# Regrouping a layer's small products on TensorE: fourteen places instead of seventeen, and two opening units in turn

## What is computed

```python
for l in range(2):
    h = rmsnorm(x)
    q, k, v, h_b, gate_b, gate_c, qc, f, i, og, zg = split(h @ w_in)      # 50 blocks of 128 columns
    ya = dilated_attention(rope(q), rope(k), v)         # 3 groups; the samples read a cache
    yb = gate_b * conv(gate_c * h_b)
    yc = gated_linear_recurrence(qc, f, i, state) ...   # HGRN2, then head norm and silu(og)
    x = x + (g0 * (ya @ w_pa) + g1 * (yb @ w_pb) + g2 * (yc @ w_pc)) @ w_o
    x = x + square(relu(rmsnorm(x) @ w_up)) @ w_down
return rmsnorm(x), and the new caches and states
```

## Time and profile before

| | |
|---|---|
| median of 3 runs | 814.51 us (814.47 to 814.7) |
| the profiled execution | 814.41 us |
| its span, first to last instruction | 812.6 us |
| busy: PE, DVE, ACT, POOL | 803.2, 559.7, 437.9, 271.8 us |
| mean granted TensorE clock | 0.997 |

### The profile page before, as it was taken

How to read it: one execution, slowest core, us unless ns; L and a number is a source line. 1 busy time by engine, 2 the same in 40 slices (tenths; PEclk the granted TensorE clock), 3 DMA queues, 4 the chain that set the end, 5 groups by cost and what they waited for, 6 DMA issues and landing times.

```text
span 812.6 us, 17682 instructions
## 1 busy us (share of the span) xinstructions
PE 803.2 (99%) x6786; PEld 790.5 (97%) x6786; DVE 559.7 (69%) x776; ACT 437.9 (54%) x625; POOL 271.8 (33%) x246
## 2 busy tenths in 40 slices
PE   8999999999999999999999999999999999999996
PEld 8999999999999999999999999999999999999996
DVE  7979777577867665554577777866787766645552
ACT  6654566545557664444354637675455666644442
POOL 3597293055700000122139825902664000001220
PEclk9999999999999999999999999999999999999998
DMA  9898899678566688767559969987765767787761
GB/s 313 236 318 295 295 262 314 188 235 318 185 210 220 219 276 291 259 238 251 187 169 232 358 212 343 262 246 232 269 221 178 252 230 251 238 284 242 250 206 53
DMA packets 171033, 199.88 MB, mean 246 GB/s; under 512 B 19680, under 2 KB 168624, under 8 KB 169648
## 3 DMA queue, kind: packets, MB, share of 16 engines
q1 hardware_dynamic: 169040, 196.48, 74.6%
q10 hardware_dynamic: 1936, 2.61, 0.9%
HBM read 191.17 MB, written 51.90 MB: 299 GB/s over the span
## 4 chain that ended last, share of the span: by engine, by line
PE 92%; POOL 3%; DVE 3%; ACT 0%; issue 0%; ACTq 0%; DVEq 0%; POOLq 0%
PE main L690 28%; PE main L691 27%; PE main L692 27%; PE small L692 1%; PE small L691 1%; PE small L690 1%; PE small L706 1%; POOL k_lv L1738 1%; POOL cum_f L1747 1%; DVE w_lo L1270 1%; PE small L735 1%; POOL suf_f L1744 1%; PE small L749 1%; DVE h_lo L1286 0%; POOL v_cache L1728 0%; PE small L782 0%
## 5 line engine op out<-in xcount | busy, mean ns | idle before, releaser
L1025 ACT ACTIVATE w_hi<-raw 128x1024 fp32r<-128x1024 f32 (+1 forms) x256 | 266.4, 1042 | 237.7 <-PE main L692 152.9
L1270 DVE TENSOR_TENSOR w_lo<-raw,w_hi 128x1024 fp32r<-128x1024 f32 (+1 forms) x256 | 330.7, 1293 | 65.5 <-ACT w_hi L1025 64.3
L690 PE MATMUL main<-h_hi,w_hi 128*128 128x264 f32 x1248 | 358.6, 287 | 0.1
L691 PE MATMUL main<-h_lo,w_hi 128*128 128x264 f32 x1248 | 353.7, 283 | 0.0
L692 PE MATMUL main<-h_hi,w_lo 128*128 128x264 f32 x1248 | 353.5, 283 | 0.0
L690 PEld LDWEIGHTS main<-h_hi,w_hi 128*128 128x128 f32 x1248 | 235.1, 188 | 4.0 <-issue 1.3
L691 PEld LDWEIGHTS main<-h_lo,w_hi 128*128 128x128 f32 x1248 | 235.2, 188 | 0.2
L692 PEld LDWEIGHTS main<-h_hi,w_lo 128*128 128x128 f32 x1248 | 234.0, 188 | 0.0
L690 PE MATMUL main<-a_hi,w_hi 128*128 128x264 f32 x512 | 145.3, 284 | 0.0
L691 PE MATMUL main<-a_lo,w_hi 128*128 128x264 f32 x512 | 145.0, 283 | 0.0
L692 PE MATMUL main<-a_hi,w_lo 128*128 128x264 f32 x512 | 145.0, 283 | 0.0
(11 more groups left out here) (241 smaller groups left out, 1035.9 us busy)
## 6 DMA issues: line engine op xcount, KB each, us to landing
raw<-in_w_in SPq DMA_DIRECT2D x48, 1024.0 KB, 6.4
raw<-in_w_up SPq DMA_DIRECT2D x32, 1024.0 KB, 5.3
raw<-in_w_down SPq DMA_DIRECT2D x32, 1024.0 KB, 5.4
out_kvs<-in_cache SPq DMA_DIRECT2D x48, 512.0 KB
out_kvs<-in_cache SPq DMA_DIRECT2D x32, 496.0 KB
raw<-in_w_o SPq DMA_DIRECT2D x8, 1024.0 KB, 5.8
raw<-in_w_br SPq DMA_DIRECT2D x8, 768.0 KB, 4.9
gates<-q_scratch SPq DMA_DIRECT2D x4, 768.0 KB, 8.0
```

The lines of the kernel that those rows point to most:

```text
L690: pe.matmul(out[:, 0:TOK], wh, rh, start=start and k == 0, stop=False)
L691: pe.matmul(out[:, 0:TOK], wh, rl, start=False, stop=False)
L1025: act.activation(w_hi[:, slot(l, u), 0:k, :], raw_of(u, k), ACT.Copy).then_inc(w_hi_ready, 1)
L1270: dve.tensor_tensor(w_lo[:, slot(l, u), 0:k, :], raw_of(u, k), w_hi[:, slot(l, u), 0:k, :].bitcast(F32), ALU.subtract).then_inc(w_lo_ready, 1)
```

## The change

The 17 places become 14: after units 8, 10, 12, 14, 17, 19, 21, 23, 25, 30, 32, 35, 37 and 39. Levels 7 and 8 move to place 17 (level 7 from 14, level 8 from 15), "values T" to place 14 and "recurrence" to place 19 (from 17). "Decayed keys T" moves from place 17 to place 21, ahead of the second half of the scores, and its copy on ACT from the turn of unit 18 to that of unit 22. Sample states, state, sample recurrence and the transposes of keys and values are regrouped at 21, 23 and 25; head norm and sample scores share place 30; the transposes of the probabilities go to 32. `TURNS` is written in the new order, so that the banks change too. The copy of "recurrence" moves from DVE (turn 18) to ACT (turn 20). `kv_outer` on DVE moves from turn 19 to turn 18. In the first layer, DVE computes the decays before `split_lo(7)`, not after it. In the second layer units 0 and 1 run in turn: seven row blocks of unit 0, seven of unit 1, then the last of each. SP's stores of the new keys and values move to match.

The diff, cut to its core:

```diff
+LEVELS_AT = ((10, (2, 3)), (12, (4, 5)), (14, (6,)), (17, (7, 8)))
 TURNS = (
     ["norm1"]
-    + ["values T", "sample values T"]
+    + ["sample values T"]
     + [f"first levels {hp} {h}" for hp in range(2) for h in range(2)]
-    + [f"level {i} {h}" for i in range(2, 9) for h in range(2)]
-    + ["recurrence", "decayed keys T", "state"]
-    + ["sample q T", "scores 0 0", "scores 1 0"]
-    + ["sample kv T 0", "sample kv T 1", "scores 0 1", "scores 1 1"]
-    + ["kv T 0", "sample states", "sample recurrence", "kv T 1", "kv T 2"]
-    + ["head norm 0", "head norm 1"]
+    + [f"level {i} {h}" for i in range(2, 7) for h in range(2)]
+    + ["values T"] + [f"level {i} {h}" for i in range(7, 9) for h in range(2)]
+    + ["recurrence", "sample q T", "scores 0 0", "scores 1 0"]
+    + ["decayed keys T", "scores 0 1", "scores 1 1", "sample states"]
+    + ["state", "sample recurrence", "sample kv T 0", "sample kv T 1"]
+    + ["kv T 0", "kv T 1", "kv T 2"]
+    + ["head norm 0", "head norm 1", "sample scores T"]
     + [f"probs T {i}" for i in range(4)]
...
 # PE
+            def opening(l):
+                for k0, nk in ((0, KT - 1), (KT - 1, 1)):
+                    for u in range(2):
...
+                        mm = unit(slot(l, u), main[bank_of(l, u)], h_hi, h_lo, k0, nk, wk0=k0, start=k0 == 0,
+                                  stop=k0 + nk == KT, per_k=per_k)
...
-                if u == 17:
+                if u == 19:
                     pe.wait_ge(masked, l * 20 + 20)
                     pe.wait_ge(far_ready, 2 * l + 2)
                     pe.wait_ge(v_tm_ready, l + 1)
...
                     done(mm, "recurrence")
+                    pe.wait_ge(roped, l + 1)
+                    transposes(l, "sample q T", [(g * P, z[:, CT_Q + g, PROMPT:TOK]) for g in range(NG)])
+                    scores(l, 0)
+                if u == 21:
                     pe.wait_ge(final_keys, l + 1)
                     transposes(l, "decayed keys T", [((tb * 2 + hp) * P, q_lv[:, 1, hp, tb * P:tb * P + P])
                                                      for tb in range(2) for hp in range(2)])
-                if u == 19:
+                    scores(l, 1)
+                    sample_states(l)
+                if u == 23:
                     pe.wait_ge(k_tm_ready, l + 1)
...
 # ACT
-                if u == 18:
+                if u == 22:
                     copy_bank(l, "decayed keys T", k_tm[:, :, :, :].rearrange("p t h c -> p (t h c)"),
                               lambda b: b[:, :], k_tm_ready)
                     freed("decayed keys T", k_tm_ready, l + 1)
                 if u == 20:
...
+                    copy_bank(l, "recurrence", o_c[:, :, 0:PROMPT], lambda b: b[:, :].rearrange("p (h t) -> p h t", h=2),
+                              o_prompt_ready)
...
 # DVE
                         if l == 0:
                             bounds()
                             new_params()
-                            split_lo(l, at + 4)
...
                         dve.sem_inc(kg_ready, 1)
+                        if l == 0:
+                            split_lo(l, at + 4)
...
                     if u == 20:
                         dve.wait_ge(bands_in, 16)
                         dve.wait_ge(k_tm_ready, l + 1)
                         mask_scores(0)
...
-                    if u in (10, 12, 14):
-                        mask_level(u - 8)
-                        mask_level(u - 7)
+                    for turn, numbers in LEVELS_AT:
+                        if u == turn:
+                            for i in numbers:
+                                if i < 8:
+                                    mask_level(i)
```

More of the change, by code:

```diff
@@ L772, in sample_rows, with keys_values @@
                 done(mm, "sample recurrence")
+            def keys_values(l, g):
+                transposes(l, f"kv T {g}", [((part * 2 + kv) * P, prompt_part(z[:, (CT_K, CT_V)[kv] + g, :], g, part))
+                                            for part in range(2) for kv in range(2)])
             def attend(l):
@@ L797, in norm1_squares @@
                 done(pe.matmul(bank[:, 0:TOK], ones, sq[:, :], start=False, stop=True), "norm1")
+            def opening(l):
+                for k0, nk in ((0, KT - 1), (KT - 1, 1)):
+                    for u in range(2):
+                        if k0 == 0:
+                            pe.wait_ge(w_lo_ready, l * UNITS + u + 5)
+                            pe.wait_ge(out_taken, l * OUTS + u + 1)
+                        per_k = None
+                        if u == 0:
+                            per_k = lambda k: pe.wait_ge(h_ready, l * 2 * KT + k0 + k + 1)
+                        elif k0 == 0:
+                            per_k = lambda k: norm1_squares(l) if k == 5 else None
+                        mm = unit(slot(l, u), main[bank_of(l, u)], h_hi, h_lo, k0, nk, wk0=k0, start=k0 == 0,
+                                  stop=k0 + nk == KT, per_k=per_k)
+                        if k0:
+                            mm.then_inc(w_used, 1)
             def between(l, u):
-                if u == 7:
+                if u == 8:
                     pe.wait_ge(consts_in, 16)
                     z_ready(pe, l, CT_CI + 1)
+                    transposes(l, "sample values T", [(hp * P, z[:, CT_CI + hp, PROMPT:TOK]) for hp in range(2)])
+                    first_levels(l)
+                for at, numbers in LEVELS_AT:
+                    if u == at:
+                        for i in numbers:
+                            level(l, i)
+                if u == 14:
                     pe.wait_ge(v_back_ready, l + 1)
@@ L844, in between @@
                     done(mm, "state")
[L845 to L850, removed]
+                    sample_rows(l)
                     z_ready(pe, l, CT_V + 2)
@@ L854, in between @@
                     transposes(l, "sample kv T 1", [(i * P, s) for i, s in enumerate(kvs[4:6])])
[L855 to L864, removed]
+                if u == 25:
+                    for g in range(NG):
+                        keys_values(l, g)
+                if u == 30:
                     pe.wait_ge(o_sq_ready, l + 1)
@@ L886, in between @@
                     done(mm, name)
+                if u == 32:
+                    pe.wait_ge(weighed, l * 4 + 4)
+                    for i in range(4):
+                        transposes(l, f"probs T {i}", [(b * P, probs[:, i // 2, i % 2, b * P:b * P + P])
+                                                       for b in range(ROW_BLOCKS)])
                 if u == 35:
@@ L926, in _ @@
                         continue
+                    if l and u < 2:
+                        if u == 0:
+                            opening(l)
+                        continue
                     if l == 0 and u < 8:
@@ L934, in _ @@
                         pe.wait_ge(out_taken, l * OUTS + n + 1)
[L935 to L940, removed]
+                        unit(slot(l, u), main[bank_of(l, n)], h_hi, h_lo, 0, KT).then_inc(w_used, 1)
                         between(l, n)
```

114 lines of the change are left out of this document (50 added, 64 removed).

## The result

The changed kernel takes 818.92 us (median of 4 executions, 817.4 to 820.67), the kernel before 814.61 us on the same chip (814.47 to 815.43). The ratio is 1.0051, with a 95% interval of 1.0038 to 1.0063: half a per cent slower. The forecast was 817.8 us, with a range of 815.8 to 819.6. The profiled execution took 817.4 us with a span of 815.6; before it was 814.41 and 812.6. So the profile has 3.0 us to explain, and the median has 1.3 us more; that rest turns out to be a cause of its own.

What follows compares the result with a forecast made beforehand. PE was taken to bound the kernel. Profiled 814.41 - 2.43 (grouping and two waits gone) + 4.28 (keys' wait) + 1.40 (masks) = 817.66, with 0.10 to the median 817.8 us; range 815.8 to 819.6.

Steps and rivals of the forecast that it cites:

- The keys' wait: At place 21, PE's scores wait for DVE's mask step, which needs ACT's keys copy: 2.14 us a layer, 4.28 in all.
- The grouping: Fewer trips between array shapes save 0.75 us a layer, 1.5 us in all; bounds 0.9 to 2.2 us in all.
- The trip that is saved: Recurrence, state and sample recurrence make two trips a layer instead of three, saving about 0.30 us of 0.42.
- The 0.45 for changes of shape: Four spots where one shape follows another without a unit between them save 0.45 us a layer.
- level 6 to values T: One change of shape without a unit between, said to save 0.1 us a layer.
- The opening and level 7: Two waits go: layer 2's unit 0 for its last row block, 0.38 us; level 7's keys, layer 1 place 14, 0.55 us.
- the decays' earlier start: In layer 1 the decays start 1.1 us earlier, named with level 7's later need for the 0.55 us saved.
- The masks: At place 19, layer 1, the recurrence waits 1.40 us for level 7's masks on DVE; no wait in layer 2.
- Rival B: Only the keys' wait shows, level 7's masks being in time: 816.4 us, chance 0.14.
- Rival D: Late DVE reaches `split_lo` or sample recurrence's bank at place 23, 1 us more a layer: 818.5 to 820 us, chance 0.10.
- the late rows of q: SP's next weights and the rows of q, queued behind `split_lo(23)`, go out some 3 us later; no cost added.
- rival E: PE's clock falls to half in each 2.1 us wait for a unit, 2.9 us more: 823.5 us, chance 0.03.

Runs made afterwards that it cites:

- The first: Changed kernel with the decayed keys transposed at the end of place 19 and ACT's copy in its turn for unit 20: 812.45 us, ratio to before 0.9973.
- third: Changed kernel with ACT copying the decayed keys three times instead of once: 822.87 us.
- fifth runs: Changed kernel with ACT's copy of the decayed keys in its turn for unit 21, ahead of `split_hi(25)`: 816.38 us.
- the eighth run: Kernel with the keys transposed at place 19, with sample recurrence moved from place 23 to the head of place 25 as its own shape: 813.37 us.
- the seventh run: Kernel with the keys transposed at place 19, with DVE's `split_lo(7)` in layer 1 ahead of the decays again: 812.69 us.
- the fourth run: Changed kernel once more with no edit: 819.29 us, ratio 1.0048; the profiled execution was the longest, 820.29 us.

## Why the prediction was right, and where it wasn't

**The keys' wait, right.** 2.27 us a layer against 2.14. Of the 0.13, 0.11 lie between the end of DVE's first `probs` step and PE: 0.21 us, where I had 0.10. The first, third and fifth runs show it from three sides: taken away, the wait gives 2.3 us a layer back; two more copies of 0.6 us add 1.26; a shorter chain takes 0.57 off.

**The grouping, right, a little large.** 0.63 us in layer 2 against 0.75. The trip that is saved was put at 0.30, and the eighth run prices one at 0.29. The 0.45 for changes of shape was a little too much, and the early places tell where. Places 7 to 15 cost 0.66 + 1.70 + 1.30 + 1.29 + 1.29 + 0.84 = 7.08 us in layer 2 before, the same products at 8 to 17 now 1.93 + 1.30 + 1.29 + 1.23 + 1.29 = 7.04: 0.04 where I had 0.1 (level 6 to values T). All later places save 0.60, where I had 0.65.

**The opening and level 7, right in size:** 0.38 and 0.60 against 0.38 and 0.55. I gave part of the credit for the second to the decays' earlier start; the seventh run shows that it had none in this, and that the new order saves 0.36 us elsewhere, in front of unit 8, which I hadn't seen.

**The masks, wrong.** The step that failed is "DVE and POOL both shift by about 1.1 us in layer 1, so they meet as before". They didn't shift alike. The 1.1 us were gone early: at 44.2 us POOL's level steps stand where they stood before (44.19 against 44.16). Later POOL's step of the earlier trace rows began 2.4 us later than before, at 73.87, and DVE's split began 0.45 us earlier, at 72.42, and was over before it, at 73.63. So the split took 1.21 us, as when alone, and not 2.96. From unit 15's last matmul to the masks' end it was 12.9 us and not 14.5, and PE came to the recurrence after 13.1, as I had it: the masks were 0.2 us early. Rival B described just this, and I had given it 0.14. That the meeting decided is read from the two traces; no run forced the two together, and with 0.2 us of slack the wait could return with a small edit.

**Two things were left out, and by luck they made up for it.** Rival D's chain ran in small: the late DVE let the rows of q out 4.0 us later, and POOL's long steps then fell on DVE's split in front of unit 29, 0.34 us. I had named the late rows of q, but gave only the weights behind them a cover; that POOL's long steps wait for these rows, and would move against DVE's splits, I didn't follow up. And rival E was true in part: not a fall in each wait at 2.9 us, but, by the times, falls in most executions at 1.5 us each. I priced a whole unit at half clock, where about half a unit ran at it. The forecast of 817.8 lies 1.1 us below 818.92: masks -1.4, clock +1.5, gap and start-up +0.5, the rest in the sizes. That the forecast came so close is owed to the first two of these cancelling.

The rule of the Trainium skill, "TensorE: Matmul & The Clock Gate", section "Why this matters for your kernels", that I set against rival E warns of idle gaps longer than these. The runs differ: 2.2 us of rest were followed by the half level in both layers of the fourth run's profile and, by the times, in many executions.

Why the same 2.20 us wait is followed by a fall in one execution and not in the next stays open; the traces show the same order of work around it to hundredths.

## What to carry to other kernels

When a small product is moved next to its consumer, ask who else waits for its copy: here PE needed a bank, that bank needed DVE, and DVE needed ACT's copy of what PE had only just produced; one place of distance took the 2.3 us a layer away and turned a loss of 4 us into a gain of 2. Merge places to save trips between array shapes (0.29 us in the eighth run) and not places of full-array products, which have no such price in the earlier trace rows. When a kernel's executions spread more than its neighbours', profile a second, longer one before explaining the median.

## What the hardware showed that I had not expected

- A rest of 2.20 us on PE was followed, 0.7 and 1.4 us after it resumed, by some 3 us at half clock in both layers of one profile of the changed kernel and in neither of the other; each fall cost 1.5 us, and by the times (816.93 to 820.67 us over ten) most executions have one or two. After 3.46 us of rest it came in both layers, in layer 1 as PE resumed and in layer 2 1.6 us later. After 1.63 us the spread of 11 executions shows none, and with matmuls in the wait that of 6 shows none.
- The clock can also fall during the last matmuls of the program, where it cost 0.58 us in the fourth run.
- At the half level the matmuls of 264 columns start 0.22 us apart instead of 0.12.
- DVE's split of 128x1024 took 1.22 us alone and up to 4.16 beside POOL's 128x1024 steps. By the rule of the Trainium skill, "SBUF — State Buffer", section "Who interferes with whom", these exclude each other, the first to start keeping the port. The row of 4.16 us agrees: the split began at 506.09, during POOL's three steps, and ended at 510.25, 1.1 us after the POOL step that follows them (508.10, 1.07 us). Layer 1's doubtful case doesn't test the rule after all: POOL's step began at 73.87, when the split of 1.21 us was over.
- Start-up varied by tenths (first unit at 6.21 us before, 6.43 after) with no edit near it.
